# Modulation product with raw fp32 weight blocks as the stationary operand, and its blocks moved to other places

## The chip, the cores and the metric

The kernel is one launch on one core of a Trainium2 chip. The time is the device time of that core in microseconds (us), from the median of the runs given. A smaller time is better. The profile is one further execution on the same kind of core, with its own time.

## The reference

A two-layer block (`DEPTH = 2`) with width 1024 works on 256 latent tokens `x` and 256 context tokens `ctx`, all in fp32. Each layer is a gated feed-forward, a mixer and a second gated feed-forward. What the change touches is the line that turns the two condition vectors `c` and `c_ctx` into 9 vectors of 1024 numbers for each layer:

```python
for i in range(DEPTH):
    mx = (jax.nn.silu(c) @ w_mod[i] + b_mod[i]).reshape(bsz, N_MOD, d)...      # w_mod[i]: 1024 x 9216
    mc = (jax.nn.silu(c_ctx) @ w_mod[i] + b_mod[i]).reshape(N_MOD, 1, 1, d)
    x   = swiglu_half(x,   mx, 0, ...)    # shift, scale, gate = m[0], m[1], m[2]
    ctx = swiglu_half(ctx, mc, 0, ...)
    ... mixer on modulate(x, norm_pre, m[3], m[4]), gate m[5]; swiglu_half with m[6], m[7], m[8]

def swiglu_half(h, m, k, g_pre, g_post, wg, wu, wd):
    u = rmsnorm(h, g_pre) * (1 + m[3*k+1]) + m[3*k]
    y = (silu(u @ wg) * (u @ wu)) @ wd
    return h + 0.5 * m[3*k+2] * rmsnorm(y, g_post)
```

So for each layer a 1024 x 9216 weight is multiplied with just two vectors, and the result is needed in pieces: the first third by the first feed-forward, the second by the mixer, the last by the second feed-forward.

## The kernel before, in words

Features lie on the partitions and the 512 tokens on the free axis. Each large weight is read in panels of 1024 x 256 (1 MB), and a panel is used as two halves of 128 output columns. For a half, ScalarE rounds the weight to fp32r (`weight_hi`, L85), VectorE (or GpSimd, L100) subtracts to get the rest (`weight_lo`, L93), and TensorE runs 8 x 3 matmuls (`product_half`, L131 to L133: high x high, high x low, low x high) with the weight block standing and 512 tokens moving (256 in the last layer's latent-only parts). The program runs in stages, each a block with its own list for every engine: the opening; then in each layer a feed-forward, the mixer's input part (`mix_in`), its output part (`mix_out`), and a second feed-forward; then the closing. There is no scheduler: each engine takes its list in the written order, and semaphores hold it.

The modulation product has 72 blocks of 128 columns a layer, 144 in all. I call one such block a **mod half**. Before the change `load_mod` brings a panel of two, `mod_hi` (ScalarE, L172) and `mod_lo` (VectorE, L178) split each into high and low, and `mod_mm` (L195) runs 8 matmuls with the condition vectors standing and the split weight moving: 256 columns each, the high and the low part. The standing operand is a 128-wide window of a mostly zero buffer `cond`, which places the result of each half in its own four rows of bank 4. When a group is finished VectorE adds the parts (`mod_rows_dve`), TensorE transposes them (`mod_turn_pe`, L214), and VectorE adds the bias (`mod_out_dve`).

The mod halves stand in the lists as follows: 16 in the opening; 44 in the gate/up loop and 12 in the down product of layer 0's first feed-forward; 44 and 24 in layer 0's second; 4 in the down product of layer 1's first. The mixers and layer 1's second feed-forward have none. `OutProduct` is the helper for the down product and for the mixer's output product. At its end stands what I call a **tail**: squares of the result are summed over the features by matmuls with fp32 data standing and a column of ones moving (`sums_pe`, L238), the reciprocal root is spread by `rstd_pe` (L275), the residual is added, and with `norm_follows` the sums are made again for the next norm (`residual_rms_pe`). `warm_pe` (L441) runs matmuls whose result nobody reads, between these steps.

Of the kernel before, what the change touches and what calls it, by code (L numbers as in the profile page):

```python
# [162 lines left out]
def load_mod(K, sp, w_mod, q, panel):  # L163

    sp.wait_ge(K.mod_lo.sem, K.mod_lo.at(2 * panel))
    sp.dma_start(K.raw_mod[:, :, :], panel_src(w_mod, 0, 8, P * q)).then_inc(K.mod_full.inc(16), 16)

def mod_hi(K, act, h, parity, panel):
    act.wait_ge(K.mod_full.sem, K.mod_full.landed(panel + 1))  # L170
    act.wait_ge(K.mod_mm.sem, K.mod_mm.at(h))
    ins = K.nc.scalar.activation(K.mod_split[:, 0], K.raw_mod[:, :, parity * P:parity * P + P], ACT.Copy)  # L172
    ins.then_inc(K.mod_hi_done.inc(), 1)

def mod_lo(K, dve, h, parity):
    dve.wait_ge(K.mod_hi_done.sem, K.mod_hi_done.at(h + 1))
    ins = K.nc.vector.tensor_tensor(K.mod_split[:, 1], K.raw_mod[:, :, parity * P:parity * P + P],  # L178
                                    r32(K.mod_split[:, 0]), ALU.subtract)
    ins.then_inc(K.mod_lo.inc(), 1)  # L180

COND_AT = P - 4

def mod_mm(K, pe, h, split, group, group_h):

    pe.wait_ge(K.mod_lo.sem, K.mod_lo.at(h + 1))
    if h == group_h and group:
        pe.wait_ge(K.mod_row.sem, K.mod_row.at(group))  # L190
    row, parity = 4 * ((h - group_h) // 2), h % 2
# [7 lines left out]
def mod_rows_dve(K, dve, h, group):  # L199

    dve.wait_ge(K.mod_mm.sem, K.mod_mm.at(h + 1))
    dve.wait_ge(K.mod_fold.sem, K.mod_fold.at(group))
    parts = K.bank[4][:, :].rearrange("p (t w n) -> p w t n", w=2, n=P)
    rows = K.rows[:, :].rearrange("p (t n) -> p t n", n=P)
    K.nc.vector.tensor_copy(rows, parts[:, 0]).then_inc(K.mod_row_hi.inc(), 1)
    dve.wait_ge(K.mod_row_hi.sem, K.mod_row_hi.at(group + 1))
    K.nc.vector.tensor_tensor(rows, rows, parts[:, 1], ALU.add).then_inc(K.mod_row.inc(), 1)

def mod_turn_pe(K, pe, group):  # L210
    pe.wait_ge(K.mod_row.sem, K.mod_row.at(group + 1))
    pe.wait_ge(K.mod_evac.sem, K.mod_evac.at(2 * group))
    for t in range(2):
        ins = K.nc.tensor.transpose(K.bank[7][:, t * P:t * P + P], K.rows[:, t * P:t * P + P], K.ident[:, :])  # L214
    ins.then_inc(K.mod_fold.inc(), 1)

def mod_out_dve(K, dve, layer, q, panels, group):

    dve.wait_ge(K.mod_fold.sem, K.mod_fold.at(group + 1))  # L220
    turned = K.bank[7][:, 0:2 * P].rearrange("p (t j i) -> p t j i", t=2, i=4)[:, :, 0:panels, :]
    out = K.mod[:, layer, q:q + 2 * panels, :].rearrange("p (j t) s -> p t j s", t=2)
    bias = K.par[:, layer, 0, q:q + 2 * panels].rearrange("p (j t) -> p t j", t=2)
    for t in range(2):
        ins = K.nc.vector.tensor_tensor(out[:, t], turned[:, t, :, 0:2], bias[:, t].unsqueeze(2).to_broadcast([P, panels, 2]), ALU.add)
    ins.then_inc(K.mod_evac.inc(), 1)
    dve.wait_ge(K.mod_evac.sem, K.mod_evac.at(2 * group + 1))
    for t in range(2):
        ins = K.nc.vector.tensor_tensor(out[:, t], out[:, t], turned[:, t, :, 2:4], ALU.add)
    ins.then_inc(K.mod_evac.inc(), 1)  # L230
# [198 lines left out]
def residual_rms_pe(K, pe, tok, y, nth, norms_before):  # L429
    warm_pe(K, 6)  # L430
# [13 lines left out]
class OutProduct:  # L444
# [6 lines left out]
    def __init__(self, K, w, parts, order, xh, xl, tok, xtok, y, halves, panels, stats, norms, next_norm, gain, mods=0,  # L451
                 mod_h=0, mod_layer=0, mod_q=0):
# [15 lines left out]
    def sp(self, sp, following):  # L468
# [1535 lines left out]
```

## Time and profile before

| | |
|---|---|
| median of 3 runs | 2396.52 us (2394.71 to 2398.04) |
| the profiled execution's own time | 2397.97 us |
| its span from first to last instruction | 2396.2 us |
| TensorE (PE) busy | 2249.7 us, 94% |
| VectorE (DVE) busy | 1229.8 us, 51% |
| ScalarE (ACT) busy | 1018.1 us, 42% |
| GpSimd (POOL) busy | 224.2 us, 9% |
| DMA | 291.06 MB, 121 GB/s on average |
| mean granted TensorE clock | 0.965 of full |

How to read it: PE is TensorE's matmuls, PEld its weight loads, which can run beside them. A record starts where its instruction starts, and matmul records overlap, so the cost of one in a dense stretch is read from start to start.
### The profile page before, as it was taken

What the parts mean: (1) busy time and instruction counts of PE and PEld (TensorE: products, weight loads), DVE (VectorE), ACT (ScalarE), POOL (GpSimd) and SP (SyncE); (2) the same over time, 40 slices, a digit from 0 to 9 for tenths busy, and PEclk for the clock granted to TensorE, in tenths of its full rate; (3) what the DMA queues carried; (4) which work ended last, traced back from release to release, by engine and by line L of the source; (5) the groups of instructions that cost most, each with busy time, mean ns of one, the idle gap of its engine ahead of it and who ended that gap; (6) DMA issues with size and microseconds to landing.
All of it is one profiled execution on the core that took longest, in us unless ns stands there. A gap on an engine that the chain in (4) does not pass through costs nothing. (4 is left out here: it accounts for less than half of the span.)

```text
span 2396.2 us, 28723 instructions
## 1 busy us (share of the span) xinstructions
PE 2249.7 (94%) x11753; PEld 1908.0 (80%) x11753; DVE 1229.8 (51%) x1679; ACT 1018.1 (42%) x1525; POOL 224.2 (9%) x139
## 2 busy tenths in 40 slices
PE   5999999998988989999999999999999988889998
PEld 5788888876676768788888788888888776779998
DVE  4544444247769743544444444333324578855554
ACT  5534433254465343544443344222324444555443
POOL 0000000023322300100000000000001332300000
PEclk8999999999999989899999998999998998989999
DMA  6454454212342213255454441333322233333553
GB/s 218 141 173 161 158 172 157 93 56 70 90 123 84 75 53 96 80 168 166 158 169 161 150 136 61 97 97 97 122 96 66 71 107 96 106 118 125 191 177 124
DMA packets 282545, 291.06 MB, mean 121 GB/s; under 512 B 8286, under 2 KB 275502, under 8 KB 282414
## 3 DMA queue, kind: packets, MB, share of 16 engines
q1 hardware_dynamic: 281619, 287.04, 37.3%
q8 instruction: 93, 1.52, 0.3%
q10 hardware_dynamic: 795, 2.18, 0.3%
q14 instruction: 38, 0.31, 0.0%
HBM read 288.02 MB, written 1.18 MB: 121 GB/s over the span
## 5 line engine op out<-in xcount | busy, mean ns | idle before, releaser
L85 ACT ACTIVATE split<-raw 128x1024 fp32r<-128x1024 f32 (+1 forms) x368 | 382.8, 1040 | 940.5 <-PE bank L133 930.9
L93 DVE TENSOR_TENSOR split<-raw,split 128x1024 fp32r<-128x1024 f32 (+1 forms) x304 | 364.8, 1200 | 714.4 <-ACT split L85 714.4
L131 PE MATMUL bank<-uh,split 128*128 128x512 f32 (+1 forms) x1344 | 488.5, 363 | 1.1 <-DVE split L93 1.1
L133 PE MATMUL bank<-uh,split 128*128 128x512 f32 (+1 forms) x1344 | 488.4, 363 | 0.0
L132 PE MATMUL bank<-ul,split 128*128 128x512 f32 (+1 forms) x1344 | 488.3, 363 | 0.0
L133 PEld LDWEIGHTS bank<-uh,split 128*128 128x128 f32 x1344 | 253.9, 189 | 40.2
L131 PEld LDWEIGHTS bank<-uh,split 128*128 128x128 f32 x1344 | 254.1, 189 | 38.5 <-issue 1.5
L132 PEld LDWEIGHTS bank<-ul,split 128*128 128x128 f32 x1344 | 254.0, 189 | 36.5
L131 PE MATMUL bank<-mix_uh,split 128*128 128x512 f32 (+1 forms) x608 | 235.4, 387 | 25.6 <-POOL split L100 15.6
L131 PE MATMUL bank<-hh,split 128*128 128x512 f32 (+1 forms) x704 | 256.6, 364 | 1.0 <-DVE split L93 1.0
L133 PE MATMUL bank<-hh,split 128*128 128x512 f32 (+1 forms) x704 | 255.7, 363 | 0.0
L132 PE MATMUL bank<-hl,split 128*128 128x512 f32 (+1 forms) x704 | 255.6, 363 | 0.0
L132 PE MATMUL bank<-mix_ul,split 128*128 128x512 f32 (+1 forms) x608 | 220.0, 362 | 0.0
L133 PE MATMUL bank<-mix_uh,split 128*128 128x512 f32 (+1 forms) x608 | 219.9, 362 | 0.0
L195 PEld LDWEIGHTS bank<-mod_split,cond 128*128 128x128 f32 x1152 | 158.6, 195 | 35.9 <-DVE mod_split L178 13.8
L100 POOL TENSOR_TENSOR split<-raw,split 128x1024 fp32r<-128x1024 f32 x64 | 153.9, 2405 | 334.0 <-ACT split L85 334.0
L178 DVE TENSOR_TENSOR mod_split<-raw_mod,mod_split 128x1024 fp32r<-128x1024 f32 x128 | 156.4, 1222 | 55.3 <-ACT mod_split L172 55.3
L195 PE MATMUL bank<-mod_split,cond 128*128 128x256 f32 x1152 | 163.7, 288 | 22.3 <-DVE mod_split L1778 11.5
L172 ACT ACTIVATE mod_split<-raw_mod 128x1024 fp32r<-128x1024 f32 x128 | 135.1, 1055 | 81.7 <-DMA raw_mod<-in_w_mod 65.0
L411 POOL TENSOR_TENSOR res<-res,y 128x512 f32<-128x512 f32 (+1 forms) x20 | 22.4, 1136 | 1542.2 <-DVE y L397 1542.0
L131 PEld LDWEIGHTS bank<-mix_uh,split 128*128 128x128 f32 x608 | 119.8, 197 | 49.0 <-issue 17.7
L131 PEld LDWEIGHTS bank<-hh,split 128*128 128x128 f32 x704 | 132.9, 189 | 21.0 <-issue 1.5
(227 smaller groups left out, 3004.8 us busy)
## 6 DMA issues: line engine op xcount, KB each, us to landing
raw_mod<-in_w_mod SPq DMA_DIRECT2D x64, 1024.0 KB, 4.8
raw<-in_ffn_w_gate SPq DMA_DIRECT2D x44, 1024.0 KB, 5.1
raw<-in_ffn_w_up SPq DMA_DIRECT2D x44, 1024.0 KB, 5.1
raw<-in_w_in SPq DMA_DIRECT2D x40, 1024.0 KB, 5.1
raw<-in_ffn_w_down SPq DMA_DIRECT2D x32, 1024.0 KB, 4.9
raw<-in_w_out SPq DMA_DIRECT2D x16, 1024.0 KB, 4.9
raw<-in_ffn_w_down SPq DMA_DIRECT2D x16, 768.0 KB, 4.3
decay<-cum_rows SPq DMA_DIRECT2D x48, 256.0 KB, 3.3
```

The lines of the kernel that those rows point to most:

```text
L85: ins = K.nc.scalar.activation(K.wh[:, half, 0:kn, :], K.raw[:, slot, 0:kn, half * P:half * P + P], ACT.Copy)
L93: ins = K.nc.vector.tensor_tensor(K.wl[:, half, 0:kn, :], K.raw[:, slot, 0:kn, half * P:half * P + P], r32(K.wh[:, half, 0:kn, :]), ALU.su ...
L100: ins = K.nc.gpsimd.tensor_tensor(K.wl[:, half, 0:kn, :], K.raw[:, slot, 0:kn, half * P:half * P + P], r32(K.wh[:, half, 0:kn, :]), ALU.su ...
L131: K.nc.tensor.matmul(bank[:, 0:tn], K.wh[:, half, k, :], h, start=first and k == 0, stop=False)
L132: K.nc.tensor.matmul(bank[:, 0:tn], K.wh[:, half, k, :], l, start=False, stop=False)
L133: ins = K.nc.tensor.matmul(bank[:, 0:tn], K.wl[:, half, k, :], h, start=False, stop=last and k == kn - 1)
L172: ins = K.nc.scalar.activation(K.mod_split[:, 0], K.raw_mod[:, :, parity * P:parity * P + P], ACT.Copy)
L178: ins = K.nc.vector.tensor_tensor(K.mod_split[:, 1], K.raw_mod[:, :, parity * P:parity * P + P], r32(K.mod_split[:, 0]), ALU.subtract)
L195: ins = K.nc.tensor.matmul(out, cond, split[:, :, k, :], start=h == group_h and k == 0, stop=True, skip_group_check=True)
L411: ins = K.nc.gpsimd.tensor_tensor(K.res[:, j, t0:t0 + tn], K.res[:, j, t0:t0 + tn], y[:, j, 0:tn], ALU.add)
```

## The change

The modulation product is turned round. The raw fp32 weight block now stands, without a split, and the two condition columns (`condf`, 128 x 2 for each of 8 input blocks) move, in full fp32. The result of a mod half is two columns with features on the partitions, so splitting, padding, folding and transposing go away, and one VectorE add puts the bias on. The order of the mod halves over the stages is new: opening 16 as before; first feed-forward of layer 0: 44 in the loop, none in the down product, 4 in its tail; mixer output of layer 0: 4 inside (after its halves 3, 3, 4 and 5) and 4 in the tail; second feed-forward of layer 0: 36 in the loop and 4 in the tail; first feed-forward of layer 1: 4 in the tail; mixer input of layer 1: 20, in pairs; mixer output of layer 1: 4 inside and 4 in the tail. The first mod half of a tail replaces three `warm_pe` matmuls ahead of the sums, the other three replace six after `rstd_pe`. In the opening the parameters' small DMAs move from SyncE's queue to ScalarE's.

```diff
+def mod_product(K, pe, w, out):
     for k in range(8):
-        cond = K.cond[:, COND_AT + P * k - row:COND_AT + P * k - row + P]
-        out = K.bank[4][:, parity * 2 * P:(parity + 1) * 2 * P].rearrange("p (w n) -> p w n", w=2)
-        ins = K.nc.tensor.matmul(out, cond, split[:, :, k, :], start=h == group_h and k == 0, stop=True, skip_group_check=True)
+        ins = K.nc.tensor.matmul(out, w[:, k, :], K.condf[:, k, :], start=k == 0, stop=k == 7, skip_group_check=True)
     ins.then_inc(K.mod_mm.inc(), 1)
...
+def mod_half(K, pe, h, bank=7, at=0):
+    full = K.mod_full[h // 2 % 2]
+    pe.wait_ge(full.sem, full.landed(h // 4 + 1))
+    mod_product(K, pe, K.raw_mod[:, h // 2 % 2, :, h % 2 * P:h % 2 * P + P], K.bank[bank][:, at + 2 * h:at + 2 * h + 2])
...
+def load_mod(K, sp, layer, q, panel):
+    sp.wait_ge(K.mod_mm.sem, K.mod_mm.at(2 * panel - 2))
...
@@ OutProduct.sp @@
         for p in range(self.n_panels):
-            if p < self.mods // 2:
-                load_mod(K, sp, K.w_mod[self.mod_layer], self.mod_q + 2 * p, self.mod_h // 2 + p)
+            if self.fill and p in (0, 3):
+                for panel in (0, 1) if p == 0 else (2, 3):
+                    load_mod(K, sp, self.mod_layer, self.mod_q + 2 * panel, panel)
...
@@ OutProduct.pe @@
-                if n < self.mods:
-                    mod_mm(K, pe, h, K.mod_split, self.mod_group, self.mod_h)
+                for h, at in enumerate(self.fill):
+                    if at == n:
+                        mod_half(K, pe, h)
...
-        warm_pe(K, 3)
+        h = self.before + len(self.fill)
+        if self.tail:
+            if self.before:
+                pe.wait_ge(K.mod_evac.sem, K.mod_evac.at(1))
+            mod_half(K, pe, h)
+        else:
+            warm_pe(K, 3)
         pe.wait_ge(K.sq_added.sem, K.sq_added.at(7))
         sums_pe(K, pe, K.sq[:, 0, :], self.tok, True, True)
-        warm_pe(K, 2)
+        warm_pe(K, 1)
         rstd_pe(K, pe, self.tok, self.norms)
+        for i in range(1, self.tail):
+            mod_half(K, pe, h + i)
...
@@ feed_forward, TensorE's gate/up loop @@
-                    if mods_loop:
-                        mod_mm(K, pe, 4 * i + half, K.mod_split, 0, 0)
+                    if 4 * i + half < mods_loop:
+                        mod_half(K, pe, 4 * i + half)
...
@@ mix_in, TensorE's list @@
+                if MODS_AT <= n < MODS_AT + mods and n % 2 == 0:
+                    pe.wait_ge(K.mod_full[0].sem, K.mod_full[0].landed((n - MODS_AT) // 2 + 1))
+                    for h in (n - MODS_AT, n - MODS_AT + 1):
+                        mod_product(K, pe, K.raw_mod[:, 0, :, h % 2 * P:h % 2 * P + P], K.bank[0][:, CTX + 2 * h:CTX + 2 * h + 2])
...
@@ hybrid_block @@
-            feed_forward(K, layer, 0, FULL, layer, 16 if layer == 0 else 68, layer == 0,
-                         12 if layer == 0 else 4, mixer_first(K, layer), (layer, 1))
+            feed_forward(K, layer, 0, FULL, layer, 40 if last else 16, 0 if last else 44, 4, mixer_first(K, layer), (layer, 1))
...
```

`MODS_AT` is the 20th half of the mixer's input product, so the ten pairs stand ahead of halves 20, 22, ..., 38, that is over the scan and the last projection (`z`).

**The opening.** TensorE's list from its start to the end of the stage; `condf,raw` and `condf,stage` are the new products (raw weight standing, two columns moving), `mod_split,cond` the old ones, `ident,xt` the transposes of the tokens, `ones,xt` the sums of squares.

```order
-L1706 MATMUL bank<-ident,cr 128x16
-L1697 MATMUL bank<-ident,pr 128x120
-L1697 MATMUL bank<-ident,pr 128x124
-L1697 MATMUL bank<-ident,pr 128x108
-L195 MATMUL bank<-mod_split,cond 128x256 x64
-L1718 MATMUL bank<-ident,xt 128x128 x32
-L238 MATMUL bank<-ones,xt 128x1 x16
-L275 MATMUL bank<-ident,rstd 128x128 x4
-L195 MATMUL bank<-mod_split,cond 128x256 x64
-L214 MATMUL bank<-ident,mod_rows 128x128 x2
+L1638 MATMUL bank<-ident,cr 128x16
+L173 MATMUL bank<-condf,raw 128x2 x32
+L1646 MATMUL bank<-ident,xt 128x128 x32
+L173 MATMUL bank<-condf,stage 128x2 x32
+L1627 MATMUL bank<-ident,pr 128x120
+L1627 MATMUL bank<-ident,pr 128x124
+L1627 MATMUL bank<-ident,pr 128x108
+L197 MATMUL bank<-ones,xt 128x1 x16
+L234 MATMUL bank<-ident,rstd 128x128 x4
+L173 MATMUL bank<-condf,stage 128x2 x64
```

Four mod halves now stand ahead of the token transposes, four between them and the sums, and eight at the end; before it was eight and eight.

**A tail, before.** TensorE's list behind the last down product of layer 0's first feed-forward (`hh`, `hl`: hidden values, high and low; `tri,ident` is `warm_pe`; `ones,sq` and `ones,y` are sums).

```order
L133 MATMUL bank<-hh,split 128x512
L441 MATMUL bank<-tri,ident 128x256 x3
L238 MATMUL bank<-ones,sq 128x1 x4
L441 MATMUL bank<-tri,ident 128x256 x2
L275 MATMUL bank<-ident,rstd 128x128 x4
L441 MATMUL bank<-tri,ident 128x256 x6
L238 MATMUL bank<-ones,y 128x1 x32
```

**The same tail in the changed kernel.**

```order
L133 MATMUL bank<-hh,split 128x512
L173 MATMUL bank<-condf,raw_mod 128x2 x8
L197 MATMUL bank<-ones,sq 128x1 x4
L389 MATMUL bank<-tri,ident 128x256
L234 MATMUL bank<-ident,rstd 128x128 x4
L173 MATMUL bank<-condf,raw_mod 128x2 x24
L197 MATMUL bank<-ones,y 128x1 x32
```

Three mod halves stand between the spreading of the root and the 32 sums that the next stage waits for; ten warming matmuls have become one.

## Rows read from the trace of the kernel before

**Rows 1.** The page, part 1: busy time, share of the span, instructions.

```profile
PE 2249.7 (94%) x11753; PEld 1908.0 (80%) x11753; DVE 1229.8 (51%) x1679; ACT 1018.1 (42%) x1525; POOL 224.2 (9%) x139
```

**Rows 2.** Busy time by stage, whole stages; columns: stretch, length, engines, PEclk, DMA, GB/s.

```profile
0.00:60.30 60.30, 34.81 (x209) 32.32 (x210) 26.06 (x34) 30.56 (x45) 2.66 (x13) 0.86 0.62 217
60.30:507.60 447.30, 442.42 (x2166) 372.97 (x2166) 201.81 (x220) 181.36 (x228) 6.28 (x5) 0.99 0.44 144
...
984.80:1451.80 467.00, 456.25 (x2262) 385.87 (x2263) 216.26 (x232) 193.62 (x240) 6.28 (x5) 0.98 0.46 151
1451.80:1845.60 393.80, 391.67 (x1748) 324.76 (x1748) 138.38 (x162) 128.38 (x176) 6.28 (x6) 0.98 0.30 94
1845.60:2111.00 265.40, 223.81 (x1271) 187.02 (x1271) 195.16 (x341) 131.55 (x230) 89.64 (x46) 0.92 0.31 96
```

**Rows 3.** Waits of PE: who for whom, us in total, times, longest.

```profile
PE bank L195 <- DVE mod_split L178: 10.8, 8, 3.1
```

**Rows 4.** Timeline of PE in a gate/up loop, layer 0: start, length, instruction.

```profile
102.23 0.39 PE L133 MATMUL bank<-uh,split 128*128 128x512 f32 x1
102.46 1.11 PE L195 MATMUL bank<-mod_split,cond 128*128 128x256 f32 x8
103.41 0.40 PE L131 MATMUL bank<-uh,split 128*128 128x512 f32 x1
```

**Rows 5.** Line L238 in 494 to 497: min/median/max ns, first and last start.

```profile
L238 PEld LDWEIGHTS bank<-ones,y x29: 192/192/193, 493.8 to 496.9; 128*128 128x128 f32 x29
```

**Rows 6.** Line L238 in 1838 to 1841, the same columns.

```profile
L238 PEld LDWEIGHTS bank<-ones,y x16: 333/333/333, 1837.7 to 1840.9; 128*128 128x128 f32 x16
```

**Rows 7.** Busy time in three short stretches, columns as in Rows 2.

```profile
80.00:82.00 2.00, 0.00 (x0) 0.00 (x0) 1.03 (x1) 1.98 (x2) 0.00 (x0) 1.00 0.00 0
494.00:497.00 3.00, 3.00 (x29) 3.00 (x29) 2.97 (x6) 2.29 (x5) 2.97 (x4) 1.00 0.00 0
499.00:502.00 3.00, 3.00 (x16) 3.00 (x16) 0.00 (x0) 0.11 (x1) 0.00 (x0) 0.50 0.00 0
```

**Rows 8.** Timeline of PE in the tail of layer 0's first feed-forward.

```profile
486.21 1.46 PE L441 MATMUL bank<-tri,ident 128*128 128x256 f32 x6
487.79 1.05 PE L238 MATMUL bank<-ones,sq 128*128 128x1 f32 x8
...
490.57 2.75 PE L441 MATMUL bank<-tri,ident 128*128 128x256 f32 x12
493.60 9.97 PE L238 MATMUL bank<-ones,y 128*128 128x1 f32 x64 [0.28 <-ACT y L424]
503.44 2.05 PE L441 MATMUL bank<-tri,ident 128*128 128x256 f32 x4
```

**Rows 9.** Timeline of PE in the tail of layer 1's mixer output.

```profile
2175.52 3.63 PE L238 MATMUL bank<-ones,mix_y 128*128 128x1 f32 x32
```

**Rows 10.** Timeline of PE in layer 0's mixer output, after its half 3.

```profile
899.70 0.50 PE L131 MATMUL bank<-out_xh,split 128*128 128x512 f32 x1 [1.87 <-DVE out_xl L1571]
```

**Rows 11.** Layer 1's mixer input: over the scan, and over the last projection; columns as Rows 2.

```profile
1955.00:2080.00 125.00, 100.71 (x615) 83.07 (x614) 102.24 (x192) 51.77 (x108) 32.18 (x20) 0.89 0.32 101
2080.00:2104.00 24.00, 22.93 (x184) 22.43 (x182) 15.52 (x19) 10.29 (x18) 14.37 (x6) 1.00 0.35 111
```

**Rows 12.** Timeline of the opening, PE and ACT.

```profile
13.57 2.00 ACT L1741 ACTIVATE mod_split<-raw 128x1024 fp32r<-128x1024 f32 x2 [5.74 <-DMA raw<-in_w_mod]
...
16.11 7.66 PE L195 MATMUL bank<-mod_split,cond 128*128 128x256 f32 x48 [8.58 <-DVE mod_split L1778]
...
26.30 3.65 PE L1718 MATMUL bank<-ident,xt 128*128 128x128 f32 x32
...
32.75 6.31 PE L238 MATMUL bank<-ones,xt 128*128 128x1 f32 x32 [2.80 <-DVE xt L247]
```

**Rows 13.** PE's groups in 16 to 19, and in 22 to 24: xcount | busy us, mean ns.

```profile
L195 PE MATMUL bank<-mod_split,cond 128*128 128x256 f32 x13 | 3.1, 426 | 8.6 <-DVE mod_split L1778 8.6
...
L195 PE MATMUL bank<-mod_split,cond 128*128 128x256 f32 x15 | 1.9, 281 | 0.0
```

More of the change, by code:

```diff
@@ L176, in mod_lo @@
[L176 to L191, printed above, removed]
+def load_mod(K, sp, layer, q, panel):
+    sp.wait_ge(K.mod_mm.sem, K.mod_mm.at(2 * panel - 2))
+    src = panel_src(K.w_mod[layer], 0, 8, P * q)
+    sp.dma_start(K.raw_mod[:, panel % 2], src).then_inc(K.mod_full[panel % 2].inc(16), 16)
@@ L235, in sums_pe, with mod_out_dve @@
+def mod_out_dve(K, dve, layer, q, h, halves, bank=7, at=0):
+    dve.wait_ge(K.mod_mm.sem, K.mod_mm.at(h + halves))
+    sums = K.bank[bank][:, at + 2 * h:at + 2 * (h + halves)].rearrange("p (j s) -> p j s", s=2)
+    bias = K.par[:, layer, 0, q:q + halves].unsqueeze(2).to_broadcast([P, halves, 2])
+    K.nc.vector.tensor_tensor(K.mod[:, layer, q:q + halves, :], sums, bias, ALU.add).then_inc(K.mod_evac.inc(), 1)
 def sums_pe(K, pe, src, tok, first, last):
@@ L717, in trip @@
                     weight_lo(K, dve, 0, 1, 8, 4 * i + 1)
-                mod(i, 0, first)
                 if not first:
@@ L728, in trip @@
                     weight_lo(K, dve, 0, 0, out.parts[0], 4 * pairs)
-                mod(i, 3, first)
                 product(i, 0)
@@ L818 @@
 LN_MEAN, LN_SQ = 34, 36
+MODS_AT = SCAN_AT + 2
 def reads(n, who):
@@ L840, with mix_in @@
 DECAYS = 4
-def mix_in(K, M, layer, last, following):
+def mix_in(K, M, layer, last, following, mod_q, mods):
     nc = K.nc
@@ L1731, in params @@
                     rows, at = PACK_ROWS[n], layer * PACKS + n
-                    act.wait_ge(K.turn.sem, K.turn.at(2 + at + (8 if layer else 0)))
+                    act.wait_ge(K.turn.sem, K.turn.at(10 + at))
                     ins = nc.scalar.activation(K.par[:, layer, n, 0:rows], K.bank[1 + at % 2][:, 0:rows], ACT.Copy)
                     ins.then_inc(K.turned.inc(), 1)
-            def mods(first):
-                for h in range(first, first + 8):
-                    full = K.raw_full[h // 2] if h < 4 else K.stage_full[h // 2 - 2]
-                    act.wait_ge(full.sem, full.landed(1))
-                    act.wait_ge(K.mod_mm.sem, K.mod_mm.at(h - 3))
-                    ins = nc.scalar.activation(split[:, h % 4, 0], raw_mod(h), ACT.Copy)
-                    ins.then_inc(K.mod_hi_done.inc(), 1)
@@ new lines, in _ @@
+            for layer in range(1, L):
+                for pack, row, src in param_rows(K, layer):
+                    dst = pr[row:row + src.shape[0], layer * PACKS + pack, :]
+                    act.dma_start(dst, src).then_inc(K.params_late.inc(16), 16)
+            for layer in range(L):
+                row = I["ssd_d"][layer].rearrange("(o h) -> o h", o=1).to_broadcast([P, 16])
+                act.dma_start(K.dload[:, layer, :], row).then_inc(K.small_in.inc(16), 16)
+                for src, dst in ((I["ssd_dt_bias"], K.dtb), (I["ssd_a_log"], K.alog)):
+                    row = src[layer].rearrange("(o d) h -> o (d h)", o=1).to_broadcast([P, 32])
+                    act.dma_start(dst[:, layer, :], row).then_inc(K.small_in.inc(16), 16)
@@ L1763, in _ @@
+            for layer in range(L):
                 params(layer)
-            mods(8)
+            rstd_act(K, act, FULL, 1024, 4, 1)
             split_ahead_act(K, act)
```

239 lines of the change are left out of this document (73 added, 166 removed).

## The prediction, made before the changed kernel was run

> **What bounds the kernel now.** I read the page first, then the busy time by stage, then PE's waits, then timelines at the places where the change puts work. PE is busy for 94% of the span, VectorE for 51%, ScalarE for 42% [rows 1]: the reader is to see that two of the three engines that the change relieves had room. By stage it is sharper. In the three long feed-forwards PE is busy for 442 of 447 us, 456 of 467 and 392 of 394, with VectorE under half; layer 1's mixer input is the loose stage, 224 of 265, with VectorE at 195; in the opening PE works 35 of 60 us [rows 2]. PE's waits for the old splits are 10.8 us over the whole program outside the opening [rows 3]. So taking the splits off ScalarE and VectorE can give back some 10 us, and what decides is what a mod half costs on PE in its old form and in its new one.
>
> **Price of the old form.** In the loop the 8 matmuls start at 102.46 and the next product at 103.41: 0.95 us a mod half, 0.119 a matmul [rows 4].
>
> **Price of the new form.** No matmul of the old kernel has two moving columns, but `sums_pe` has the same shape with one: a 128x128 fp32 block stands and one column moves. It shows as two records a product, each with its own weight load. At the full clock 29 loads start within 3.1 us: 28 gaps, 0.11 us each [rows 5], with PEclk at 1.00 and PEld busy all of the time [rows 7]. At the half clock 16 loads take 3.2 us: 0.213 each [rows 6]. The gap doubles with the clock, so it is array time and not issue time. The weight loads set it; one column or two makes no difference that I can see. A mod half is 8 products, so 16 loads: 16 x 0.11 = **1.76 us at the full clock, 3.41 at the half**. That is 0.81 us more than the old form at the full clock. The bounds: below, nothing of the load is seen because it hides beside other matmuls (a rival, below); above, 3.41.
>
> The Trainium skill has two rules for this, in "TensorE: Matmul & The Clock Gate". The section "LDWEIGHTS (loading the stationary operand)" gives a load's time as its columns divided by 1.2 GHz, 107 ns for 128 columns, whatever moves behind it; 16 of them make an estimate of 1.71 us, and the measured 0.11 agrees. The section "Back-to-back issue gap" gives a matmul of 1 to 64 columns a floor of some 25 ns, which would be an estimate of 0.4 us a half, less than the old form; the loads of 0.11 speak against it.
>
> **Feed-forwards without their tails.** The stage of layer 1's first feed-forward is 393.8 us with 4 old mod halves [rows 2]; without them 390.0. New layer 0, first: 390.0 + 44 x 1.76 = 467.4 against 447.3, **+20.1**. Layer 0, second: 390.0 + 36 x 1.76 = 453.4 against 467.0, **-13.6** (its down product loses 24 halves, and the waits of its start go too). Layer 1, first: **-3.8**. Layer 1, second: 0. Together +2.7. This takes the clock as staying full. The low-column stretch is 1.76 us between products of 24 x 0.227 = 5.4 us; and at 80 to 82 PE stood idle for two whole microseconds with the clock at 1.00 [rows 7]. A fall would come on top (rival A).
>
> **The five tails.** The new list puts three mod halves between the spread root and the 32 sums, which the next stage waits for. Before, the root was spread by 490.57, where six warming products start, and 64 loads of sums went from 493.60 to 503.57 [rows 8]. In them the clock fell: 1.00 at 494 to 497, 0.50 at 499 to 502 [rows 7]. Now the low-column stretch begins at 486.2 already, with one warming product in it, so the clock falls earlier: the three mod halves cost 3 x 1.76 = 5.3 (full) to 10.2 (half), the sums 64 x 0.213 = 13.6. From 490.6 that ends at 509.5 to 514.4, against 503.6: +5.9 to +10.8. I take +8.5, the middle. Layer 1's mixer output has half the sums, 3.63 us at the full clock [rows 9]; they become 32 x 0.213 = 6.8 and the three halves come ahead, nearly the same sum. 5 x 8.5 = **+42.5** (30 to 54). If the clock stayed full, 490.6 + 5.3 + 7.1 = 503.0, no change. The first mod half, 1.76, replaces three warming products of 1.46 [rows 8] ahead of a sum that waits for VectorE until 487.8: nothing.
>
> **The eight halves inside the mixer outputs.** 8 x 1.76 = 14.1. PE idles 1.87 us after half 3 of layer 0's [rows 10], and about as much in layer 1's, which hides some 3. Two in a row make 3.5 us with few columns, which may lower the clock: +1. **+12** (10 to 18).
>
> **The twenty in layer 1's mixer input.** They go in pairs. Over the last projection (8 halves) PE is busy for 22.9 of 24 us [rows 11]: 8 x 1.76 = 14.1 in full. Over the scan (12 halves, 21.1 us) PE is free for 24 of 125 us and VectorE busy for 102 [rows 11]; what is free is spread over waits of the scan's chain, so I hide half, +10.5. The clock is already at 0.89 on average there, and each pair may lower it: +3. **+27** (10 to 45).
>
> **The opening.** The old products ran on a cold array first: 426 ns a record at 16 to 19, 281 at 22 to 24 [rows 13], so the old products, with 256 columns each, brought the clock up. The sums, with one, did not hold it [rows 7], and I expect no more of two. The first panel landed at 13.57 [rows 12]; with six small DMAs and a memset fewer ahead, I put it at 12. Then at the half clock: 4 halves to 25.7; token transposes 3.65 [rows 12] to 7, say to 32; 4 halves to 45.6; parameters 2; 32 loads of sums 6.8; root and spread 3; 8 halves 27.3: 84.7, and one add and the gain make 86. Against 60.3, +25; the transposes may bring the full clock for a few microseconds, so **+22** (-9 to +25; -9 is the same chain at the full clock, where 16 halves cost 28 us and it ends near 51). The sums' waits there are hidden in it. The splits that go hide nothing: PE is now what the opening ends on.
>
> The parameter DMAs on ScalarE's queue come before its first activation, but that has some 12 us until the first panel lands. In the loops SyncE's `load_mod` now waits for PE to be through the second last mod half, and the next weight panel is queued behind it; the split into that buffer needs the same product and then 1.0 us on ScalarE alone [rows 12] and VectorE's part, which is about a mod half, so I cost it at nothing. Where it doesn't hold, a panel comes late by up to a mod half, 1.8 us, at 20 places: +36 at most.
>
> **Sum.** 2.7 + 42.5 + 12 + 27 + 22 = +106 on the profiled 2397.97 us, 2504; the median of the runs lies 1.45 under that execution, so **2503 us**.
>
> **Rivals.**
> A. The clock falls inside the loops as well. For it: a loop has a low-column stretch every 7.2 us, and in the mixer, with PE 80% busy, the clock is 0.89. Against: it held over an idle stretch of 2 us. At worst each of the 80 loop halves costs 3.41 in place of 1.76, +132: 2635. If a quarter do, +33: 2536.
> B. The clock does not fall, since PE has no gaps. For it: PE's records are unbroken in such stretches. Against: they were unbroken at 499 to 502 too, at 0.50. It takes the 42.5 of the tails, and turns the opening from +22 to -9: 2430.
> C. The kernel gets faster: the weight loads hide as they do in the large products, where 512 columns take 0.227 and 256 take 0.119, so that 2 columns come to some 0.011 us a record and 0.18 a half. Then the 128 halves outside the opening save 0.77 each, 98 us, and the waits of rows 3 go: 2396.5 - 98 - 11 = 2287. The point from which it decides is 0.95 us a half, or 0.059 a load; the loads of the sums were 0.11 with nothing else running, so almost half would have to vanish. It is the "gap" rule of the skill, too.
> D. The placement works: what stands in the mixers and beside VectorE's waits is hidden, so 39 us become some 10: 2474.
>
> **Chances.** Forecast (2455 to 2550) 0.72 with D in it; A beyond that 0.12; B 0.10; C 0.04, and 0.02 for a result near the old time from several terms at their low ends. The range that should hold 8 in 10 is 2440 to 2550. Runs of this kernel differ by some 0.1%, so 0.2%, 5 us, is what can be told from no change: faster 0.05, same 0.01, slower 0.94.
>
> **What would show it.** PE's new group (line 173) should have 2304 records, in a loop 16 in about 1.76 us, and a trip half of 7.2 us in place of 6.4. In the tails PEclk should be 0.50 before the sums start, and they should run at 0.213. The opening should end at 80 to 86, with PE busy from 12 on. In the mixer of layer 1 the stage should be 10 to 45 us longer. VectorE and ScalarE should lose busy time in the loops without any of it showing in the span. A mod half that takes under 1 us in a loop would make the whole forecast wrong; a PEclk of 1.00 through the tails and the opening would make it 70 us too high.

## The result and the profile after

The changed kernel takes **2534.9 us** (median of 3 runs, 2528.4 to 2534.95) against 2396.52. The ratio over all runs is put at 1.0565, 95% interval 1.0547 to 1.0583. It is slower by 138 us, where +106 was forecast; the time lies inside the range. The profiled execution's span is 2533.0 us, and the mean granted clock fell from 0.965 to 0.934.

The page's part 1 answers to [rows 1]:

```profile
PE 2425.5 (96%) x12791; PEld 2093.0 (83%) x12791; DVE 1052.1 (42%) x1507; ACT 872.0 (34%) x1380; POOL 222.3 (9%) x138
```

VectorE lost 178 us of work and ScalarE 146; PE gained 176 us. PE's idle time fell from 146.5 us (2396.2 less 2249.7) to 107.5, so at most 39 us of what the two engines lost can have helped. The busy time by stage, columns as in [rows 2]:

```profile
0.00:79.40 79.40, 65.92 (x335) 64.86 (x336) 6.07 (x12) 14.94 (x28) 1.67 (x12) 0.72 0.48 165
79.40:563.10 483.70, 482.75 (x2462) 413.91 (x2463) 132.91 (x154) 124.27 (x172) 6.31 (x6) 0.96 0.37 124
914.10:1051.50 137.40, 134.95 (x646) 116.86 (x646) 49.46 (x70) 47.20 (x76) 6.28 (x5) 0.86 0.28 92
1051.50:1518.90 467.40, 465.46 (x2334) 397.30 (x2335) 132.89 (x154) 124.30 (x172) 6.29 (x5) 0.96 0.36 120
1518.90:1918.50 399.60, 397.69 (x1759) 331.81 (x1759) 132.71 (x154) 124.39 (x172) 6.36 (x6) 0.96 0.29 92
1918.50:2231.70 313.20, 279.34 (x1591) 244.05 (x1591) 194.97 (x342) 131.72 (x231) 88.62 (x46) 0.86 0.36 115
2231.70:2319.00 87.30, 83.98 (x583) 82.71 (x583) 37.19 (x71) 35.58 (x68) 3.56 (x5) 0.81 0.44 145
```

Two things are to be seen. The feed-forwards are bounded by PE (busy 482.75 of 483.70 us). And PEclk, the column before the last two, is lower in every stage in which new halves stand: 0.86 to 0.72 in the opening, 0.92 to 0.86 in layer 1's mixer input. In a loop a mod half looks like this (timeline of PE; answers to [rows 4]):

```profile
124.32 0.39 PE L133 MATMUL bank<-uh,split 128*128 128x512 f32 x1
124.55 1.84 PE L173 MATMUL bank<-condf,raw_mod 128*128 128x2 f32 x16
126.25 0.49 PE L131 MATMUL bank<-uh,split 128*128 128x512 f32 x1
```

From 124.55 to 126.25 it is 1.70 us, 0.106 a record, where the old form took 0.95. The tail of layer 0's first feed-forward answers to [rows 8]:

```profile
530.26 1.84 PE L173 MATMUL bank<-condf,raw_mod 128*128 128x2 f32 x16
531.96 1.03 PE L197 MATMUL bank<-ones,sq 128*128 128x1 f32 x8
532.85 0.68 PE L389 MATMUL bank<-tri,ident 128*128 128x256 f32 x2
533.62 1.74 PE L234 MATMUL bank<-ident,rstd 128*128 128x128 f32 x8
535.15 10.24 PE L173 MATMUL bank<-condf,raw_mod 128*128 128x2 f32 x48
545.25 13.79 PE L197 MATMUL bank<-ones,y 128*128 128x1 f32 x64
...
563.11 1.19 PE L389 MATMUL bank<-tri,ident 128*128 128x256 f32 x2 [0.44 <-PEq L520]
```

The three halves take 10.1 us (0.21 a record) and the sums 13.7. The clock had fallen ahead of both, though PE stood still for only 0.09 us (busy time, same columns):

```profile
530.00:533.00 3.00, 3.00 (x27) 2.93 (x26) 0.69 (x1) 2.53 (x4) 0.00 (x0) 1.00 0.00 0
533.00:536.00 3.00, 2.91 (x15) 2.50 (x15) 0.71 (x2) 2.24 (x4) 0.00 (x0) 0.67 0.00 0
536.00:539.00 3.00, 3.00 (x16) 3.00 (x15) 2.97 (x6) 1.42 (x3) 2.75 (x3) 0.50 0.01 3
```

The opening answers to [rows 12]:

```profile
11.85 13.78 PE L173 MATMUL bank<-condf,raw 128*128 128x2 f32 x64 [6.92 <-DMA raw<-in_w_mod]
25.49 5.32 PE L1646 MATMUL bank<-ident,xt 128*128 128x128 f32 x32
30.65 9.06 PE L173 MATMUL bank<-condf,stage 128*128 128x2 f32 x64
...
41.70 6.86 PE L197 MATMUL bank<-ones,xt 128*128 128x1 f32 x32
...
50.99 27.30 PE L173 MATMUL bank<-condf,stage 128*128 128x2 f32 x128
79.40 1.19 PE L389 MATMUL bank<-tri,ident 128*128 128x256 f32 x2 [1.11 <-PEq L1571]
```

The last eight halves are one stretch at 0.213 a record. What the prediction did not have is a pair of halves at the head of each long loop, behind the interleaved first products (timeline of PE):

```profile
97.73 4.26 PE L173 MATMUL bank<-condf,raw_mod 128*128 128x2 f32 x32
101.84 0.77 PE L131 MATMUL bank<-uh,split 128*128 128x512 f32 x1
...
103.27 0.63 PE L131 MATMUL bank<-uh,split 128*128 128x512 f32 x1
...
104.55 0.63 PE L131 MATMUL bank<-uh,split 128*128 128x512 f32 x1
```

Behind it the large product runs at the half clock until 107: its k-steps (the three matmuls of one input block) are 1.28 us apart instead of 0.69. The same happens in the mixer input of layer 1, where such pairs are the rule. One pair there, 32 records, starts at 2183.09 (busy time):

```profile
2180.00:2183.00 3.00, 3.00 (x26) 2.85 (x24) 3.00 (x9) 2.70 (x3) 1.59 (x1) 1.00 0.00 0
2183.00:2188.00 5.00, 4.97 (x36) 4.92 (x36) 3.95 (x5) 1.36 (x3) 3.20 (x2) 0.81 0.02 3
2188.00:2192.00 4.00, 4.00 (x21) 4.00 (x20) 0.00 (x0) 0.00 (x0) 0.00 (x0) 0.50 0.86 282
```

### The profile page after: what moved, and what is told of

The parts are those of the page before. It is cut to its first block and busy times, and to the rows that moved or that the text cites. A ratio compares the mean times of both kernels' runs of the same rounds, so it can differ in the third digit from the quotient of the medians.

```text
span 2533.0 us, 30323 instructions
## 1 busy us (share of the span) xinstructions
PE 2425.5 (96%) x12791; PEld 2093.0 (83%) x12791; DVE 1052.1 (42%) x1507; ACT 872.0 (34%) x1380; POOL 222.3 (9%) x138
## 5 line engine op out<-in xcount | busy, mean ns | idle before, releaser
L131 PE MATMUL bank<-uh,split 128*128 128x512 f32 (+1 forms) x1344 | 498.3, 371 | 1.1 <-DVE split L93 1.1
L133 PE MATMUL bank<-uh,split 128*128 128x512 f32 (+1 forms) x1344 | 490.0, 365 | 0.0
L131 PE MATMUL bank<-mix_uh,split 128*128 128x512 f32 (+1 forms) x608 | 238.6, 392 | 20.1 <-POOL split L100 14.3
L133 PE MATMUL bank<-mix_uh,split 128*128 128x512 f32 (+1 forms) x608 | 222.9, 367 | 0.0
L173 PEld LDWEIGHTS bank<-condf,raw_mod 128*128 128x128 f32 x1472 | 192.4, 206 | 6.3
L173 PE MATMUL bank<-condf,raw_mod 128*128 128x2 f32 x1472 | 184.0, 256 | 0.0
L131 PEld LDWEIGHTS bank<-hh,split 128*128 128x128 f32 x704 | 132.8, 189 | 22.1 <-issue 1.5
L133 PEld LDWEIGHTS bank<-hh,split 128*128 128x128 f32 x704 | 132.9, 189 | 20.6
L132 PEld LDWEIGHTS bank<-hl,split 128*128 128x128 f32 x704 | 132.9, 189 | 20.5
```

Source lines behind the costliest of these rows:

```text
L131: K.nc.tensor.matmul(bank[:, 0:tn], K.wh[:, half, k, :], h, start=first and k == 0, stop=False)
L132: K.nc.tensor.matmul(bank[:, 0:tn], K.wh[:, half, k, :], l, start=False, stop=False)
L133: ins = K.nc.tensor.matmul(bank[:, 0:tn], K.wl[:, half, k, :], h, start=False, stop=last and k == kn - 1)
L173: ins = K.nc.tensor.matmul(out, w[:, k, :], K.condf[:, k, :], start=k == 0, stop=k == 7, skip_group_check=True)
```

## Experiments

Two theories stood after the comparison: (1) a product costs its weight loads, at whatever width moves behind them; (2) it is the few moving columns, not gaps, that let the clock fall, so a large part of the loss is clock and not work. The rivals: the moved columns cost, a half has a fixed price, or the places and waits of the halves cost the time. In the experiments "two columns" is the changed kernel's product and "wide" one with 128 moving columns. Length of every stage in the profiled executions, us; the last row is the median of the timed runs (one run for e8):

| stage | before | changed | e1 | e2 | e3 | e4 | e5 | e6 | e7 | e8 | e9 | e10 |
|---|---|---|---|---|---|---|---|---|---|---|---|---|
| opening | 60.3 | 79.4 | 57.5 | 79.6 | 79.7 | 60.6 | 56.5 | 54.6 | 82.7 | 56.2 | 79.4 | 79.5 |
| layer 0, first ff | 447.3 | 483.7 | 471.0 | 483.9 | 477.5 | 450.0 | 444.6 | 465.9 | 482.3 | 435.9 | 481.7 | 482.4 |
| mixer input 0 | 352.9 | 351.0 | 352.8 | 350.3 | 350.8 | 350.3 | 350.8 | 350.8 | 350.6 | 356.3 | 353.6 | 352.9 |
| mixer output 0 | 124.3 | 137.5 | 131.1 | 143.1 | 138.0 | 126.7 | 120.6 | 125.1 | 137.4 | 128.3 | 140.1 | 143.0 |
| layer 0, second ff | 467.0 | 467.4 | 455.2 | 463.0 | 465.1 | 467.1 | 461.8 | 451.5 | 467.2 | 425.9 | 465.6 | 463.0 |
| layer 1, first ff | 393.8 | 399.6 | 391.7 | 439.4 | 397.9 | 395.7 | 389.1 | 386.8 | 399.4 | 394.5 | 399.8 | 396.7 |
| mixer input 1 | 266.2 | 313.2 | 284.7 | 263.3 | 313.4 | 264.7 | 262.3 | 284.4 | 325.1 | 280.3 | 296.4 | 287.2 |
| mixer output 1 | 70.5 | 87.3 | 78.6 | 86.7 | 85.6 | 71.9 | 71.6 | 77.5 | 86.7 | 78.3 | 83.7 | 87.5 |
| median | 2396.5 | 2534.9 | 2438.7 | 2526.7 | 2520.4 | 2403.6 | 2377.6 | 2420.0 | 2546.4 | 2371.9 | 2514.6 | 2502.9 |

Layer 1's second feed-forward is 214 us in all. Between mixer output 0 and the stage behind it some 5 us move back and forth in kernels that are alike there (137.5 + 467.4, 143.1 + 463.0), so these two are best read as a sum. The lines of the diffs below are those that matter; `...` marks what is left out.

### e1: 128 moving columns in every product

```diff
+COLS = 128
...
-        ins = K.nc.tensor.matmul(out, w[:, k, :], K.condf[:, k, :], start=k == 0, stop=k == 7, skip_group_check=True)
+        ins = K.nc.tensor.matmul(out, w[:, k, :], K.condf[:, 2 * k:2 * k + COLS], start=k == 0, stop=k == 7, skip_group_check=True)
...
+            nc.gpsimd.memset(K.condf[:, 16:], 0.0).then_inc(K.const_step.inc(), 1)
...
```

Only the first two columns of each result are read; the rest is overwritten by the next half. At most 16 of the 128 moved columns hold numbers, the others are zeros.

> The changed kernel with 128 moving columns instead of 2 in every conditioning product (the two condition columns, then other finite columns whose sums nothing reads); loads, order and places are unchanged. Theory: a product takes what its sixteen weight loads take, and the low level of the clock comes from stretches in which TensorE moves few columns. Then a half in a loop stays at 1.7 to 1.85 us (0.11 a record), TensorE stays at 1.00 in the mixer's pairs, behind the loop's first pair, in the opening's and the tails' products, and the time falls by 50 to 85 us, to 2450 to 2485. Rival 1, the moved columns cost: 128 of them come on top of each load, a half takes 2.6 us or more, and the time rises by 80 us or more. Rival 2, the clock falls for another reason, such as the place of the products: the clock is as before and the time within 5 us of the changed kernel's.

Measured: 2438.7 us (2436.0 to 2439.23), ratio to before 1.0169 (1.0154 to 1.0185). 96 of the 138 us are gone with 64 times the columns and the same loads. A record takes 0.11 us as before in the loop, and now in the tail too:

```profile
99.28 1.95 PE L176 MATMUL bank<-condf,raw_mod 128*128 128x128 f32 x16
...
507.49 5.52 PE L176 MATMUL bank<-condf,raw_mod 128*128 128x128 f32 x48
512.85 11.54 PE L200 MATMUL bank<-ones,y 128*128 128x1 f32 x64
```

The three halves take 5.4 us instead of 10.1. PEclk stays 1.00 through the tail up to the one-column sums, and falls in these with PE busy all of the time:

```profile
509.00:512.00 3.00, 3.00 (x29) 3.00 (x29) 2.97 (x6) 1.82 (x3) 3.00 (x3) 1.00 0.00 0
512.00:515.00 3.00, 3.00 (x31) 3.00 (x29) 2.83 (x6) 1.95 (x4) 2.84 (x3) 1.00 0.00 0
515.00:518.00 3.00, 3.00 (x17) 3.00 (x17) 0.00 (x0) 1.03 (x2) 0.00 (x0) 0.53 0.03 5
```

Both theories hold and both of their rivals fall. The gain is above the 50 to 85 expected; 22 us of it are the opening, now shorter than before the change (57.5 against 60.3).

### e2: the mixer's twenty halves in a loop

```diff
-        mix_in(K, M, layer, last, w_out_first, 44, 20 if last else 0)
+        mix_in(K, M, layer, last, w_out_first, 44, 0)
...
-            feed_forward(K, layer, 0, FULL, layer, 40 if last else 16, 0 if last else 44, 4, mixer_first(K, layer), (layer, 1))
+            feed_forward(K, layer, 0, FULL, layer, 40 if last else 16, 20 if last else 44, 4, mixer_first(K, layer), (layer, 1))
```

> The changed kernel with the twenty halves of layer 1's mixer input moved into the loop of layer 1's first feed-forward, one behind each of its first twenty halves. Theory: twenty single halves cost 1.85 us each there, some 37 us, with 1 to 2 us for the pair at the loop's start, and the mixer input gives back the 47 us that it lost, because its clock no longer falls behind each pair: 6 to 10 us faster than the changed kernel. Rival: the 20 us that the mixer input lost beyond its loads were not the clock but waits on its single buffer or its scan; then its idle rows before the products go, and the clock stays as low there as before. Rival 2: a half costs the same wherever it stands, no difference above 3 us.

Measured: 2526.7 us (2525.12 to 2533.01), ratio 1.0544 (1.0527 to 1.056): 8 less than the changed kernel, spans 10 less. The loop's stage grew by 39.8, 1.99 a half with the dip at its head; the mixer input gave back 49.9. With two moving columns the mixer was the dearer place; e10 shows why.

### e3: no half in the tails

The list in brackets now names the halves of the down or output product behind which a mod half stands. The tails have the warming matmuls of the kernel before again.

```diff
-                         lambda dve: post_gain_dve(K, dve, layer, 1, 1.0), layer, 64, 0, (3, 3, 4, 5), 4)
+                         lambda dve: post_gain_dve(K, dve, layer, 1, 1.0), layer, 64, 0, (3, 3, 4, 5, 9, 10, 12, 13))
...
-            feed_forward(K, layer, 0, FULL, layer, 40 if last else 16, 0 if last else 44, 4, mixer_first(K, layer), (layer, 1))
+            feed_forward(K, layer, 0, FULL, layer, 40 if last else 16, 4 if last else 44, () if last else (6, 9, 12, 15), mixer_first(K, layer), (layer, 1))
...
-            feed_forward(K, layer, 2, LATENT if last else FULL, layer + 1, 0, 0 if last else 36, 0 if last else 4, after,
+            feed_forward(K, layer, 2, LATENT if last else FULL, layer + 1, 0, 0 if last else 40, (), after,
```

> The changed kernel with no half in the five tails: those of layer 0's first feed-forward stand singly between halves of its down product, those of its second and of layer 1's first in their loops, those of the two mixer outputs as four more fills; the tails have the warm matmuls of the kernel before (3, 2, 6). Theory: in the tail three halves at half clock take 10 us and the sums behind them 14 instead of 10; between dense halves a half costs 1.85 us and no clock. Tails give back about 48 us, the twenty halves cost 37: 8 to 14 us faster. Rival: a tail's halves stand in time in which TensorE waits for the squares anyway, so that moving them out gives back less than they cost: 0 to 25 us slower.

Measured: 2520.4 us (2516.12 to 2523.74), ratio 1.0511 (1.0495 to 1.0528): 14 less than the changed kernel, spans 11 less, about the 8 to 14 expected. The twenty halves cost less where they went, so in the tails they were not hidden behind the wait for the squares.

### e4: the kernel before, wide warming products between the sums

```diff
         sums_pe(K, pe, y[:, j, :], tok, n == 0, n == 7)
+        if n in (1, 3, 5):
+            warm_pe(K, 1)
```

> The kernel before with one 256-column warm matmul behind the second, fourth and sixth of the eight sums of each tail (layer 0's and 1's four tails with a next norm, and the second mixer output's). Theory: it is the eight sums of one moving column that let the clock fall in the tail (1.00, then 0.73, 0.50 in rows of the kernel before); with wide matmuls between them the clock stays, sums and next products run at 0.11 a record, and each tail gets 1 to 2.5 us shorter: 5 to 12 us faster than the kernel before. Rival: the clock falls all the same, and three warm matmuls on the chain of the sums cost 0.55 to 1.1 us each: 6 to 15 us slower.

Measured: 2403.6 us (2402.55 to 2406.34), ratio 1.0034 (1.0021 to 1.0047): slower by 6 us, as the rival had it. The clock fell within these stretches, as in the kernel before (0.64 over 497 to 500), with PE busy throughout:

```profile
497.00:500.00 3.00, 3.00 (x19) 2.82 (x18) 1.16 (x2) 1.75 (x3) 1.22 (x1) 0.67 0.00 0
500.00:503.00 3.00, 3.00 (x13) 2.90 (x14) 0.00 (x0) 0.00 (x0) 0.00 (x0) 0.50 0.00 0
```

So three products of 256 columns between the 64 one-column records did not hold it here, and they stood on the chain.

### e5: the kernel before, the sums themselves 128 columns wide

```diff
-        ins = K.nc.tensor.matmul(K.bank[5][:, t:t + 1], src[:, t * P:t * P + P], K.ones[:, 0:1],
+        ins = K.nc.tensor.matmul(K.bank[5][:, t * P:t * P + P], src[:, t * P:t * P + P], K.ones[:, :],
                                  start=first and t == 0, stop=last, skip_group_check=True)
...
```

The square root reads column 0 of each 128.

> The kernel before with 128 moving columns of ones instead of one in every sum (the 128 sums of a row are equal, the square root reads the first), in bank 5 at 128t instead of t. Theory from the wide products: a record takes its load, 0.11 us, whatever moves up to 128 columns, and it is the one-column records that let the clock fall in the tails and in the opening. Then the 64 records of a tail's sums take 7.1 us instead of 10 and what follows runs at 1.00, 3 to 4.5 us in each of four tails, 1 to 2 in the last mixer output's and 2 to 4 in the opening: 12 to 25 us faster than the kernel before. Rival: the clock falls in the tail because of TensorE's waits for the squares, or because the sums stand as 64 single records whatever they move; then nothing changes, within 5 us. Rival 2: the wide writes delay the reads of the bank, slower.

Measured: **2377.6 us** (2373.1 to 2381.32), ratio 0.9929 (0.9916 to 0.9942). It beats both kernels. The tail, against [rows 8]:

```profile
490.52 7.41 PE L238 MATMUL bank<-ones,y 128*128 128x128 f32 x64 [0.28 <-ACT y L424]
497.77 1.03 PE L441 MATMUL bank<-tri,ident 128*128 128x256 f32 x4
498.64 1.05 PE L275 MATMUL bank<-ident,rstd 128*128 128x128 f32 x8
501.09 3.26 PE L441 MATMUL bank<-tri,ident 128*128 128x256 f32 x14 [1.40 <-PEq L578]
```

```profile
494.00:497.00 3.00, 3.00 (x30) 3.00 (x29) 0.79 (x2) 1.39 (x3) 0.86 (x1) 1.00 0.00 0
497.00:500.00 3.00, 2.69 (x21) 2.34 (x19) 1.73 (x3) 0.26 (x1) 0.00 (x0) 1.00 0.00 0
```

The 64 records take 7.25 us instead of 9.84, what follows them runs at the full clock, and the tail is 18.0 us long instead of 21.4. This is theory 2 alone, in a kernel without the change.

### e6: both wide

e1 and e5's edits together.

> The changed kernel with 128 moving columns both in the conditioning products and in the sums. Theory: TensorE's clock stays at 1.00 nearly everywhere; the sums behind a tail's halves take 7.1 us instead of 11.5 to 13.8, the matmuls behind them their full-clock time: 5 tails by 4 to 6 us and 1 to 2 in the opening below the wide products alone (2438.7), so 2408 to 2422. It stays above the kernel before by the loads: 144 halves in dense places cost 0.8 us more each than two rounded matmuls a block did. Rival: with the products already wide the sums add nothing, within 4 us of 2438.

Measured: 2420.0 us (2412.43 to 2421.18), ratio 1.0097 (1.008 to 1.0114), inside the 2408 to 2422 expected; mean clock 0.99. So with the clock kept, the changed kernel is still 42 us above e5, the kernel before with the same wide sums. The two differ by the change alone, its form and its places (with 128 columns moving).

### e7: the mixer's halves one by one

```diff
-                if MODS_AT <= n < MODS_AT + mods and n % 2 == 0:
+                if MODS_AT <= n < MODS_AT + mods:
                     pe.wait_ge(K.mod_full[0].sem, K.mod_full[0].landed((n - MODS_AT) // 2 + 1))
-                    for h in (n - MODS_AT, n - MODS_AT + 1):
-                        mod_product(K, pe, K.raw_mod[:, 0, :, h % 2 * P:h % 2 * P + P], K.bank[0][:, CTX + 2 * h:CTX + 2 * h + 2])
+                    for h in (n - MODS_AT,):
+                        mod_product(K, pe, K.raw_mod[:, 0, :, h % 2 * P:h % 2 * P + P], K.bank[h % 2][:, CTX + h - h % 2:CTX + h - h % 2 + 2])
...
```

Odd halves write bank 1.

> The changed kernel (two moving columns) with the twenty halves of layer 1's mixer input one by one, ahead of each of twenty products, instead of two ahead of each of ten; those ahead of odd products write bank 1. Theory: sixteen low-column records between dense products leave the clock at 1.00, thirty-two let it fall; so the stage loses its stretches at half clock behind the pairs and takes 285 to 300 us instead of 313, 13 to 28 us faster than the changed kernel. Rival 1: the low-column scan matmuls that stand between the products let the clock fall with single halves as well: within 5 us. Rival 2: the waits of a single half for its panel now stand twice as often, slower.

Measured: 2546.4 us (2545.41 to 2547.44), ratio 1.0631 (1.0611 to 1.0652), 11 above the changed kernel: the theory's forecast failed here, and it went the way of rival 2. The stage is 12 us longer at the same mean clock and the same work:

```profile
1919.60:2244.70 325.10, 279.52 (x1591) 241.19 (x1591) 194.85 (x343) 131.81 (x230) 88.68 (x46) 0.86 0.34 111
```

PE's idle time in it rose from 33.9 to 45.6 us. Of the 11.7, 5.0 are waits for the single panel buffer, which the changed kernel didn't have, and 5.6 a longer wait of the scan (it was 1.8; waits of PE: who for whom, us, times, longest):

```profile
PE bank L966 <- DVE decay L1220: 7.4, 3, 3.8
...
PE bank L173 <- DMA raw_mod_mix<-in_w_mod: 5.0, 3, 2.4
```

Breaking up the pairs did not keep the clock. "A pair lets it fall and a single half doesn't" is right in the feed-forward's loop, where 5.4 us of 512-column products stand between, and wrong here. Products of 256 columns and the scan's of 64 stand between here, but no run shows that this is the reason.

### e8: half of the loads

```diff
-    for k in range(8):
-        ins = K.nc.tensor.matmul(out, w[:, k, :], K.condf[:, k, :], start=k == 0, stop=k == 7, skip_group_check=True)
+    for k in range(4):
+        ins = K.nc.tensor.matmul(out, w[:, k, :], K.condf[:, k, :], start=k == 0, stop=k == 3, skip_group_check=True)
```

The kernel leaves out half of each modulation sum, so its time alone is of use.

> The changed kernel with four of the eight contraction blocks in each conditioning product; the other four are left out of the sums. Theory: the price is the number of weight loads, so a half in a loop takes 0.9 us instead of 1.7 to 1.85 and a trip of the loop returns to about 6.45 us; the pairs have sixteen records and leave the clock at 1.00. 80 halves of the loops give back 68 us, the mixer input 30, tails 20, opening 12 to 15: 2395 to 2415. Rival: the price is fixed by half, such as a wait for the panel or a break in TensorE's stream between products: a half still takes above 1.3 us and the time is above 2450.

Measured: 2371.9 us, one run, below the 2395 to 2415 expected. In the loop:

```profile
88.24 0.95 PE L173 MATMUL bank<-condf,raw_mod 128*128 128x2 f32 x8
89.05 0.49 PE L131 MATMUL bank<-uh,split 128*128 128x512 f32 x1
...
94.64 0.95 PE L173 MATMUL bank<-condf,raw_mod 128*128 128x2 f32 x8
```

0.81 us a half and 6.40 from one to the next, against 1.70 and 7.28. Eight records fewer are 0.89 us, 0.11 each again: the price is by the record and not by the half. The time is below the forecast mainly by the opening, 23 us shorter where 12 to 15 were expected, and by the three feed-forwards: they are 94 shorter together, and their 80 halves in the loops, at 0.89 each, are only 71 of it.

### e9: 32 columns

e1 with `COLS = 32`.

> The changed kernel with 32 moving columns in every conditioning product. 2 columns gave 2535, 128 columns 2438.7. Theory A, a little width is enough to keep the clock: within 10 us of 2439. Theory B, what counts is the share of the record's time in which columns move, so that 32 stay low like 2: above 2520. Between these: the clock falls later in a stretch and the stages with long stretches (opening, tails) keep most of their loss, 2460 to 2510.

Measured: 2514.6 us (2513.09 to 2516.14), ratio 1.0489 (1.0459 to 1.052): 20 of the 96 us that 128 columns gave. 17 of them are layer 1's mixer input, where PEclk is 0.91, between 0.86 and e10's 0.96:

```profile
1920.20:2216.50 296.30, 263.44 (x1591) 230.18 (x1591) 192.30 (x342) 131.94 (x230) 89.07 (x46) 0.91 0.38 122
```

The opening and the tails were as with two columns. None of the three cases forecast holds as written; it lies between A and B, just above the last one's 2510.

### e10: 128 columns in layer 1's mixer input alone

e1's edit for those twenty halves only.

> The changed kernel with 128 moving columns in the twenty halves of layer 1's mixer input alone; all others move two. Theory: the 20 us that this stage took beyond the load price are the clock that falls behind pairs with two columns; the stage takes 285 us instead of 313 and the kernel 25 to 32 us less than the changed one, 2503 to 2511, all other stages as they were. Rival: the stage was slowed by the scan and the single buffer, and the gain seen there with all products wide came from elsewhere: the stage stays above 305.

Measured: 2502.9 us (2497.51 to 2508.19), ratio 1.044 (1.0381 to 1.0499), 32 less than the changed kernel and spans 27 less, as the theory said; the stage:

```profile
1917.50:2204.70 287.20, 251.61 (x1591) 217.78 (x1591) 192.23 (x342) 131.93 (x230) 89.20 (x46) 0.96 0.39 126
```

The records, the places and the buffer are those of the changed kernel; PEclk is 0.96 for 0.86, and 26 us are gone. Of the 47 us that this stage had gained 21 are left. Twenty halves are 34 us of loads (20 x 1.70), so the mixer hides 13 of them: 1.05 us a half. With the clock held it is the cheaper place, and not the dearer one as in e2.

## Why the prediction held, and where it was off

**The price of the new form.** 1.76 us a half was forecast, 1.70 measured in the loops and 3.4 at the half clock. The trip half of 7.28 us is 0.85 above the 6.43 of the kernel before (102.46 to 108.89), where 0.81 was forecast. That the load sets it, and not the column, was read from sums of one column; e1 (64 times the columns, same record) and e8 (half the records, half the time) show it. The Trainium skill, "TensorE: Matmul & The Clock Gate", section "LDWEIGHTS (loading the stationary operand)", gives a load's time as its columns divided by 1.2 GHz, 107 ns for 128 columns. The 0.106 to 0.11 of these rows agree with it at the full clock; at the half clock a load took 0.213. Rival C, that loads hide, is dead: the point it needed was 0.059.

**Feed-forwards without tails.** +2.7 forecast, +10.2 measured (+25.0, -10.6, -4.2; the tails begin at 530.26, 1486.02 and 1885.49, before at 486.21, 1429.81 and 1822.60). What was missing is above all the pair at the head of each long loop, about 3 us each (0.7 in the halves, 2.4 in the product behind): I looked at the halves one by one and not at what stands next to them in the list. Rival A is this in small; inside the loops the clock stayed at 1.00.

**The tails.** 5 x 8.5 = 42.5 forecast; measured from their first instruction to the next stage +11.4, +7.0, +10.9, +10.0 and +9.6 = 48.9. I took the middle between the halves at the full and at the half clock. In the three feed-forwards they ran at the half clock from their start (535.15), the top end of that range. In the mixer outputs the clock fell later, in the middle of them:

```profile
1027.78 6.05 PE L173 MATMUL bank<-condf,raw_mod_out 128*128 128x2 f32 x48
...
2300.34 8.60 PE L173 MATMUL bank<-condf,raw_mod_out 128*128 128x2 f32 x48
```

That is 5.9 and 8.5 us to the sums, against 10.1. The mechanism was right and the term too small.

**Inside the mixer outputs.** +12 forecast, 13.4 measured (13.2 + 16.8 less those two tails).

**Layer 1's mixer input.** +27 forecast, **+47.0** measured, just over the upper bound: this is the step that was off. Of the +27 I had put 24 on loads that don't hide and 3 on the clock. e10 takes 26 us away with the clock alone and leaves +21. So the loads, and what hides of them behind the scan's waits, were sized well, and the clock's part was nearly nine times what I had put down. The row that should have warned me was 0.89 on average over the scan [rows 11]: the clock was falling there already without the new halves.

**The opening.** +22 forecast, +19.1 measured; by its steps: panel at 11.85 (12), token transposes 5.3 (7), second four halves 9.1 (13.6; the clock had risen during the transposes and was at 0.97 over 30 to 36), last eight 27.3 (27.3).

**SyncE and VectorE's queues at nothing.** From the start of layer 0's first feed-forward to its tail PE waited 1.5 us in all, and in its second 1.8, for no panel and no weight split. Right.

**Rivals B and D.** B's 2430 is nearly what e1 measured, 2438.7, with the products wide. In part that is luck: by stage e1 misses B's terms by 3 to 9 us each way (the opening -2.8 for -9, layer 1's mixer input +18.5 for +27), and its clock still falls in the sums. D is out: it wanted 39 us in the mixers down to 10, and 60 were measured. The tails hid nothing (e3), and the mixer hid 13 of 34 us (e10), about what the forecast had taken off already.

The sum of the terms: 19.1 + 10.2 + 48.9 + 13.4 + 47.0 - 1.9 (layer 0's mixer input) = 136.7, against 136.8 between the spans. The terms' errors hardly cancel: all but the opening's (and layer 0's mixer input, which had none) were too small, and layer 1's mixer input alone makes 20 of the 32 us that the forecast missed. By cause: the 96 us of the 138 that e1 takes away are clock, in products whose loads and places did not change. The other 42, which e6 against e5 gives as well, are a balance. The 128 halves outside the opening load for 96 us more than the old form took (0.75 each, an estimate from 1.70 and 0.95); against it stand the waits and warming matmuls that went and what the mixer hides, which no run separates.

## What to carry to other kernels

Where a fp32 block stands and only a few columns move, the load is the price, and 32 or 128 columns cost no more than 2 here. So if such products stand in a row, widen what moves (e1 let zeros follow, and the results that nobody reads were overwritten) before moving the products about. Before narrow matmuls go anywhere, read PEclk there, and look at what stands beside them in the list: with two columns a half cost 1.70 us between 512-column products and 2.35 (47.0 / 20) in the mixer, with 128 columns 1.05 there (21.0 / 20). And the first gain was in neither place: the kernel before with wide sums (e5) is faster than every complete kernel with the change. The work was moved from two half-idle engines to the one that bounds, and it showed as time.

## What the runs showed of the hardware

- The clock fell from 1.00 to 0.53 and on to 0.50 with TensorE busy for all of a stretch (3.00 of 3.00 us from 512 to 518 in e1), where it moved one column a record. In the three halves of the same tail it was at 0.50 with two columns (536 to 539) and with 32 (e9, 538 to 541), and at 1.00 with 128 (e1, 509 to 512). The Trainium skill, "TensorE: Matmul & The Clock Gate", section "HAM oscillation — how this bites in real kernels", tells of gaps in the engine's work as what lets the clock fall. In the stretches shown here there were next to none (0.09 us in one), so the measurement goes beyond it.
- With three 256-column products among the 64 one-column records of a tail the clock fell all the same (e4, 0.67 and 0.50); with 128 columns in each of the 64 it stayed at 1.00 (e5).
- PEclk is not to be trusted at the start of the program: it reads 1.00 where the 64 records from 11.85 to 25.49 take 0.213 each, the half-clock figure of the last eight halves. There the records decide.

```profile
12.00:26.00 14.00, 14.00 (x67) 14.00 (x68) 0.00 (x0) 0.00 (x0) 0.00 (x0) 1.00 0.78 252
```
